# Fourteen column tiles of a gated unit laid between the steps of a paged sample attention

## The reference

```python
def decoder_layer(x, p, pos, past, lam_init, ...):
    h = rmsnorm(x, g_mix)
    z = h @ w_in
    q = z[..., :QK_COLS].reshape(B, T, N_HEADS, 2, HEAD_DK)
    ...
    gate_s = jax.nn.sigmoid(z[..., U_END + D_MODEL:])
    ...
        k_past, v_past, h0 = past
        segments = [(k_past, v_past, past_pos), (k, v, pos)]
    att = diff_attention(q, pos, segments, lam)
    att = rmsnorm(att, g_head) * (1.0 - lam_init)
    branch_a = att.reshape(B, T, ATTN_WIDTH) @ w_attn_up

    y_ssm, h_re, h_im = s5_scan(u, h0, ...)
    glu = jax.nn.gelu(y_ssm.reshape(B, T, SSM_WIDTH)) @ w_glu
    branch_s = glu[..., :D_MODEL] * jax.nn.sigmoid(glu[..., D_MODEL:])

    x = x + (gate_a * branch_a + gate_s * branch_s) @ w_out
    x = x + peer_ffn(...)
    x = x + (p @ w_ple) * jax.nn.sigmoid(rmsnorm(x, g_ple) @ w_ple_gate)
```

## Time and profile before

| | us |
|---|---|
| median of 3 runs (4792.35 to 4802.76) | 4796.71 |
| span of the profiled execution | 4793.1 |

### The profile page before, as it was taken

One profiled execution on the slowest core, in us unless ns is written; L12 is line 12 of the kernel. 1 busy time (PEld: TensorE's weight loads), 2 busy tenths in 40 slices (PEclk: granted clock), 3 DMA queues, 4 the chain that ended last, 5 costly groups with the idle time before them and its releaser, 6 DMA issues. The chain is left out here.

```text
span 4793.1 us, 80957 instructions
## 1 busy us (share of the span) xinstructions
PE 4433.3 (92%) x29778; PEld 4169.2 (87%) x29778; DVE 2599.0 (54%) x4336; ACT 1526.1 (32%) x2325; POOL 2545.3 (53%) x1827
## 2 busy tenths in 40 slices
PE   7999968998789898999999999999799999999999
PEld 6888857886379897999988999899799999999889
DVE  4477755453152302679565656555466666666631
ACT  3122214442143323223333333333333333333242
POOL 5688832321034342445566666666566666666543
PEclk9999978998789999999999999999899999999999
DMA  3222222336934432223688988878888888878532
GB/s 110 74 94 94 94 62 89 109 106 229 377 108 134 141 127 68 97 97 130 206 308 310 320 316 310 312 264 311 303 310 325 314 320 313 315 291 321 218 103 93
DMA packets 360238, 985.53 MB, mean 206 GB/s; under 512 B 43218, under 2 KB 120786, under 8 KB 301170
## 3 DMA queue, kind: packets, MB, share of 16 engines
q1 hardware_dynamic: 275138, 566.67, 34.7%
q0 software_dynamic: 47088, 339.37, 18.7%
q10 hardware_dynamic: 37824, 76.99, 4.2%
HBM read 901.03 MB, written 81.82 MB: 205 GB/s over the span
## 5 line engine op out<-in xcount | busy, mean ns | idle before, releaser
L2577 PE MATMUL val_y_ps<-val_wt,val_v 128*128 128x384 f32 x6144 | 1105.3, 338 | 39.2 <-DVE val_wt L2651 21.4
L247 PE MATMUL rt_acc<-xn_act,rt_w_hi 128*128 128x384 f32 x4096 | 1075.0, 343 | 64.0 <-POOL rt_w_rest L237 63.2
L2577 PEld LDWEIGHTS val_y_ps<-val_wt,val_v 128*128 128x128 f32 x6144 | 1065.7, 188 | 78.1 <-DVE out_xT L2675 56.4
L237 POOL TENSOR_TENSOR rt_w_rest<-rt_w_raw,rt_w_hi 128x512 fp32r<-128x512 f32 x576 | 743.4, 1311 | 562.4 <-ACT rt_w_hi L232 559.2
L247 PEld LDWEIGHTS rt_acc<-xn_act,rt_w_hi 128*128 128x128 f32 x4096 | 745.6, 190 | 87.8 <-POOL rt_w_rest L237 84.2
L2539 POOL TENSOR_TENSOR val_v<-val_v_raw,val_v 128x2048 fp32r<-128x2048 f32 x128 | 590.3, 4612 | 367.1 <-ACT val_v L2610 367.1
L247 PE MATMUL rt_acc<-xn_act,rt_w_rest 128*128 128x384 f32 x2048 | 697.0, 340 | 0.0
L232 ACT ACTIVATE rt_w_hi<-rt_w_raw 128x512 fp32r<-128x512 f32 x576 | 345.6, 630 | 494.4 <-DMA rt_w_raw<-in_peer_uT 329.5
L2454 DVE CUSTOM_DVE_ANT_0 rt_space<-rt_space,rt_mid 128x2048 f32<-128x2048 f32 x160 | 361.4, 2280 | 241.8 <-DMA rt_space<-in_peer_u,out_row_id 234.8
L2675 DVE TENSOR_TENSOR out_xT<-out_xT,val_y_ps 128x384 f32<-128x384 f32 x512 | 277.0, 551 | 376.6 <-PE val_y_ps L2577 376.6
L2610 ACT ACTIVATE val_v<-val_v_raw 128x2048 fp32r<-128x2048 f32 x128 | 245.4, 1918 | 583.6 <-PE val_y_ps L2577 551.6
(11 more groups left out here) (404 smaller groups left out, 7234.4 us busy)
## 6 DMA issues: line engine op xcount, KB each, us to landing
rt_w_raw<-in_peer_uT SPq DMA_DIRECT2D x512, 256.0 KB
val_v_raw<-in_peer_vp SPq DMA_DIRECT2D x128, 1024.0 KB, 4.9
scan_w_raw<-in_w_in SPq DMA_DIRECT2D x128, 256.0 KB, 3.0
pages_V<-in_cache_v SPq DMA_DIRECT2D x64, 512.0 KB, 11.8
att_w_raw<-in_w_in SPq DMA_DIRECT2D x96, 256.0 KB, 3.3
hid_scratch<-rt_hid ACTq DMA_DIRECT2D x128, 192.0 KB
gate_scratch<-rt_space ACTq DMA_DIRECT2D x12, 2048.0 KB
val_hid<-hid_scratch SPq DMA_DIRECT2D x32, 768.0 KB
```

The source lines that it names most:

```text
L237: e.tensor_tensor(self.rest[:, s, 0:nk, :], self.raw[:, s, 0:nk, :], self.hi[:, s, 0:nk, :].bitcast(F32), ALU.subtract).then_inc(self.rest ...
L247: mm = e.matmul(acc[:, h, 0:width], w[:, s, k, :], act[:, kt0 + k, a, col + h * width:col + (h + 1) * width], start=first and k == 0 and w ...
L2577: mm = e.matmul(y_ps[:, t % 2, 0:DW], v[:, c % 2, a, j, t * P:(t + 1) * P], wt[:, g % 2, j, b, :], start=j == 0 and a == 0 and b == 0, sto ...
```

## The change

The gated unit's products for column tiles 0 to 13 leave the mix stage and go between the steps of the sample attention; only tiles 14 and 15 (GLU_LATE = 2) stay. `stage_attention_sample` becomes `stage_sample_and_state`. Tile 0 goes ahead of the loop, each of its first six passes takes two tiles, the seventh one. In detail:

- The y tiles are read and split at the head of this stage, in a ring of four (`y_raw`), and later the same four buffers hold two gate tiles and two result tiles. `ys` outlives the stage.
- The two products of a tile now come as GATE, then VALUE, into one accumulator `acc`. ScalarE frees it after GATE (`open_gates`), VectorE after VALUE (`state_part`), both by `acc_free`. The scores lose their second buffer in PSUM for it.
- Weight units are issued by SP between the pages, in an order written out by hand, and split by ScalarE between its steps of the attention (`hi(u)` for unit u; unit u belongs to product u // 2).
- Keys and values share three buffers of 4 MB (`k.pages`) where there were four. Set 0 is the keys of sequence 0, then keys and values of the following sequences take turns; set m lies in buffer m % 3.
- The result of each early tile (128 x 544, 272 KB) is stored to `part_dram` and comes back in the mix stage (`load_back`) for its ATT product.
- The mix stage makes GATE 14, VALUE 14, GATE 15, VALUE 15 and then the 16 ATT products. All eight heads are normalised during the first four products, two heads in each (PAIRS = 4), and ATT 0 waits for them.

```diff
+GLU_LATE = 2
+GLU_EARLY = KT - GLU_LATE
...
+        y_raw = s.sb("y_raw", [P, 4, TOK])
+        gate, part = y_raw[:, 0:2], y_raw[:, 2:4]
+        ys = k.ys
+        S = s.ps("S", [P, 2, 512])
...
+        acc = s.ps("acc", [P, 2, 512])
...
+        def tiles(n):
+
+            return [2 * n + 1, 2 * n + 2] if n < NB - 2 else [2 * n + 1]
...
+        def keys_set(n):
+            return 2 * n - 1 if n else 0
+
+        def values_set(n):
+            return 2 * n + 2 if n < NB - 1 else 2 * n + 1
...
+            def load_y(t):
+                if t >= 4:
+                    e.wait_ge(y_rest, t - 3)
...
+            for t in range(4):
+                load_y(t)
+            for u in range(RING):
+                load_unit(u)
+            for t in range(4, CT):
+                load_y(t)
+            load_keys(1, range(NPG))
+            load_gate(0)
+            load_new(0)
+            load_values(0, range(NPG))
+            load_unit(4)
+            load_gate(1)
+            e.wait_ge(s_done, 1)
+            load_keys(2, range(0, 4))
+            load_unit(5)
+            load_keys(2, range(4, 8))
+            load_unit(6)
+            load_unit(7)
+            for n in range(NB - 1):
+                e.wait_ge(s_done, n + 2)
+                u = 8 * n + 4
+                load_unit(u + 4)
+                load_values(n + 1, range(0, 4))
+                load_unit(u + 5)
+                load_values(n + 1, range(4, 8))
+                if n:
+                    load_gate(2 * n + 1)
+                load_unit(u + 6)
+                load_unit(u + 7)
+                e.wait_ge(pv_done, n + 1)
+                load_new(n + 1)
+                load_unit(u + 8)
+                load_unit(u + 9)
+                if 2 * n + 2 < GLU_EARLY:
+                    load_gate(2 * n + 2)
+                if n + 3 < NB:
+                    load_keys(n + 3, range(0, 4))
+                load_unit(u + 10)
+                if n + 3 < NB:
+                    load_keys(n + 3, range(4, 8))
+                load_unit(u + 11)
...
+                e.wait_ge(acc_free, p + 1)
+                for v in range(U):
+                    w.multiply(e, 0, 0, p * U + v, acc, ys, v * UNIT, v == 0, v == U - 1)
...
+            e.wait_ge(y_rest, CT)
+            state_product(GATE, 0)
+            turn_weights(0)
+            state_product(VALUE, 0)
+            for n in range(NB - 1):
+                early, late = tiles(n)[0], tiles(n)[1:]
+                scores(n + 1)
+                state_product(GATE, early)
+                values(n)
+                state_product(VALUE, early)
+                turn(n)
+                for c in late:
+                    state_product(GATE, c)
+                turn_weights(n + 1)
+                for c in late:
+                    state_product(VALUE, c)
+            values(NB - 1)
...
+            def open_gates(c):
+                w.wait_used(e, 0, 0, (product(GATE, c) + 1) * U)
+                if c >= 2:
+                    e.wait_ge(part_stored[c % 2], 16 * (c // 2))
+                e.activation(halves(part[:, c % 2, :]), acc[:, :, 0:HALF], ACT.Sigmoid).then_inc(part_sig, 1)
+                e.wait_ge(part_sig, c + 1)
+                e.sem_inc(acc_free, 1)
+                e.wait_ge(gate_div, c + 1)
+                e.activation(gate[:, c % 2, :], gate[:, c % 2, :], ACT.Sigmoid).then_inc(gate_sig, 1)
...
+            for u in range(2):
+                hi(u)
+            for t in range(CT):
+                e.wait_ge(y_in[t % 4], 16 * (t // 4 + 1))
+                e.activation(ys[:, t, 0, :], y_raw[:, t % 4, :], ACT.Copy).then_inc(y_hi, 1)
+            hi(2)
+            hi(3)
+            exponents(0)
+            hi(4)
+            hi(5)
+            e.wait_ge(y_rest, CT)
+            open_gates(0)
+            copy_weights(0)
+            hi(6)
+            hi(7)
+            for n in range(NB - 1):
+                early, late = tiles(n)[0], tiles(n)[1:]
+                u = 8 * n + 4
+                exponents(n + 1)
+                store(early - 1)
+                hi(u + 4)
+                hi(u + 5)
+                open_gates(early)
+                copy_rows(n)
+                hi(u + 6)
+                hi(u + 7)
+                for c in late:
+                    hi(u + 8)
+                    store(early)
+                    hi(u + 9)
+                    open_gates(c)
+                copy_weights(n + 1)
+                for c in late:
+                    hi(u + 10)
+                    hi(u + 11)
...
+            def state_part(c):
+                w.wait_used(e, 0, 0, (product(VALUE, c) + 1) * U)
+                e.wait_ge(part_sig, c + 1)
+                x = halves(part[:, c % 2, :])
+                ch.step(e.tensor_tensor(x, acc[:, :, 0:HALF], x, ALU.mult))
+                e.sem_inc(acc_free, 1)
...
+        for c in range(GLU_EARLY, KT):
+            order += [(GATE, c), (VALUE, c)]
+        order += [(ATT, c) for c in range(KT)]
+        PAIRS = len(order) - KT
...
+        def load_back(e, c):
+            if c < GLU_EARLY:
+                if c >= 2:
+                    e.wait_ge(mix_ready, c - 1)
+                e.dma_start(back[:, c % 2, :], k.part_dram[c]).then_inc(back_in[c % 2], 16)
...
+            for n, (part, c) in enumerate(order):
+                if n == PAIRS:
+                    e.wait_ge(att_ready, NH)
+                e.wait_ge(part_read[n % 3], n // 3 + 1)
                 for v in range(U):
...
+                    if n < PAIRS:
+                        square_sum(n * U + v)
+                    w.multiply(e, 0, 0, n * U + v, acc[n % 3], k.att if part == ATT else ys, v * UNIT, v == 0, v == U - 1)
...
+                if n < PAIRS:
+                    for h in (n * U, n * U + 1):
+                        deviation(h)
+                        square(h + 2)
+                        if h:
+                            head_hi(h - 1)
+                elif n == PAIRS:
+                    head_hi(NH - 1)
```

359 lines of the change are left out of this document (197 added, 162 removed).

## The result

The changed kernel takes 4830.4 us (median of 6 runs, 4825.2 to 4835.5) against 4797.2 for the kernel before (6 runs on the same chip): 1.0067 of its time, 95% interval 1.0056 to 1.0078. It is slower by 0.7%, where 4766 us and "faster" had been predicted, and the time lies outside the range. The profiled span is 4823.4 us against 4793.1.

A forecast was written before the change was run, and what follows sets the result against it. Sample attention was taken as bound by pages, the mix stage by TensorE; new stage 318 us plus mix stage 152.6 make 470.6 against 501.2, 30.6 less, so 4766.1 us, range 4745 to 4790.

The forecast's parts named there:

- What bounds the kernel: Sample attention bound by page traffic at 408 GB/s, mix stage by TensorE; the new stage turns from DMA-bound to TensorE-bound.
- Start of the new stage: Sample attention up to the second scores: 55 us, with TensorE standing some 18 us before VALUE 0.
- A+47: Forecast start of VALUE 0, 47 us after the stage's start A (1150.8 us), once unit 5 has landed and been split.
- One sequence: Each of six sample-attention passes: 12.8 us of attention plus four products of 6.0, 36.8 us; with 0.8 of wait, 37.6.
- (1): In each sequence, ScalarE's second split waits for a unit issued behind four value pages; TensorE loses 0.8 us.
- (2): In each sequence, the gate tile behind all eight pages delays the output rows' copy; covered with 0.2 us to spare.
- K1: Keys of sequence 1; before the change, 4.19 MB took 13.9 us from issue at 1151.55 to first use at 1165.45.
- ScalarE's chain is later: Rival for the sequences: pages a tenth slower, waits grow, 3 us in each of seven, 4787 us; 15 in 100.
- TensorE's clock falls inside a sequence: Rival: 3.3 us lost per clock fall, 4792 us if once in each of eight sequences, 4819 if twice; eight in 100.
- A rule against the order on ScalarE: Two table loads per sequence at 1.28 us without the skill page's 1380 ns drain, which would add an estimated 11 us.
- The mix stage's head: Eight heads' norms on VectorE, 4.93 us each, first reciprocal at 7.9, delay the first attention product to 54.6 us.
- The output tiles: Sixteen attention products at 6.0 us plus 2.0 for the clock, 98 us; the wait for mix_ready costs nothing.

The follow-up runs named there:

- start_in_need: unit_and_gate_first with the start's gates opened before splits, and weight units 4 to 13 and gates issued ahead of later pages: 4775.7 us, 0.9951.
- unit_and_gate_first: Changed kernel with each turn's second weight unit and early gate tile both issued ahead of the value pages on SyncE: 4801.0 us, 1.0006.
- unit_first: Changed kernel with only each turn's second weight unit issued ahead of four value pages on SyncE: 4829.1 us, 1.0061.
- deviation_early: Changed kernel with the first root of the heads' norm ahead of the first four splits on ScalarE: 4833.1 us, 1.0070.
- all_orders: both_lists plus start units 4 to 9 ahead of later pages, first gates before splits, and two sums and roots first at the mix head: 4770.2 us, 0.9945.
- head_ordered: both_lists with the mix head's first root ahead of the splits and each next head's sum and root moved one slot earlier: 4765.6 us, 0.9938.
- gate_first: Changed kernel with the mix stage's gate sigmoid ahead of the splits for two tiles later, on ScalarE alone: 4806.5 us, 1.0016.
- back_later: Changed kernel with the mix stage's gate and part loads issued behind the next tile's weight loads, on SyncE alone: 4803.9 us, 1.0007.
- both_lists: Changed kernel with the edits of back_later and unit_and_gate_first together: 4774.7 us, 0.9951.

## Why the prediction was wrong

**What bounds the kernel: right.** The stage of the sample attention was bound by pages, the waits for pages are gone, and laid out well the sequences run at TensorE's speed.

**Start of the new stage: right in kind, 3 us short.** VALUE 0 starts at A+49.2 (A+47 was said), TensorE idle for 19.9 us before it, ScalarE released by unit 5 (1200.22, table load 1200.87, sigmoid 1202.16). I took this idle time as given, because the lists stood so in the diff; start_in_need shows that it was the order of the lists and not the 11.6 MB.

**One sequence: the step that failed is waits (1) and (2).** Both were found and both were sized with the 408 GB/s of a window inside a burst, from its first byte, and with nothing but the bytes issued ahead. The burst begins at 262 GB/s for 5 us, and 0.7 MB more than those bytes had moved when the unit was there. The unit behind four pages was split 11.6 us after the end of scores (1268.87 less 1253.19 and 4.05), where 8.9 had been said, and the sigmoid behind the gate tile began at 18.2 (1275.47), where 15.7 had been said. That turned 0.8 us of wait into 2.3 to 3.5. The rest is the clock, which the sum had at nothing here: it falls to 0.50 in or just behind each of these waits, and VALUE then takes 7.5 to 8.8 us instead of 6.0. The six waits are 16.1 us, and the six sequences are 27.7 us longer than the 224.5 of unit_and_gate_first: the other 11.6 are the clock. The slow start could have been read before: the prediction's own row of K1 has 4.19 MB in 13.9 us, where 2 us and 408 GB/s give 12.3. The prediction said of (2) that anything beyond its 0.2 us to spare would be paid six times; unit_first showed exactly that, once (1) no longer stood in front of it.

**The rivals.** The second, "ScalarE's chain is later", is what happened in this stage, with its reason nearly as given: 26.6 us against its 21. It had 15 in 100, but the argument against it (the DMA engines have been idle before each burst) didn't hold: behind such a pause the rate is 262 GB/s and not 408. The third, "TensorE's clock falls inside a sequence", came about in part, 1.4 to 2.8 us in each, but not by itself: in unit_and_gate_first the same small matmuls stand between the same products, and the clock is 1.00 for 225 us. What pulled it down was the wait. The changed kernel's mean over the six sequences is 0.95, just at the limit that the prediction had named as the sign of this rival. The Trainium skill (TensorE: Matmul & The Clock Gate, HAM oscillation) describes this loss for a loop whose waits come back in each pass; the trace agrees, with 0.80 in the wait and 0.50 behind it.

**A rule against the order on ScalarE: weighed rightly.** The table loads in the new stage take 1.28 us and stand 0.02 us behind the split (1269.52 behind 1268.87 and 0.63). The drain of 1380 ns for each switch that the Trainium skill gives (ScalarE: Activation LUTs, What ACT_TABLE_LOAD costs) shows in none of the rows.

**The mix stage's head: right, 3 us short.** 57.9 against 54.6. A head's pitch on VectorE was 5.05 us, not 4.93, and the first reciprocal started 9.9 us in, not 7.9, because ScalarE waited for the third and fourth unit before the first root. deviation_early, all_orders and head_ordered bear out the chain: it is moved only when all three engines' lists move.

**The output tiles: the step that failed outright.** "The unit behind the wait for mix_ready still lands 3 us before its split's result is wanted: nothing." For TensorE alone that holds: in gate_first, where SyncE's list is as it was, TensorE is busy for 99.39 of the tiles' 99.40 us. But the split is not only work for TensorE's sake: on ScalarE the opening of the gate stands behind it, and the addition that SyncE waits for stands behind that. I followed the added wait to the engine that multiplies and stopped there, instead of asking who else stands behind each instruction that it delays. It costs 22.7 us on 98, nearly a quarter; in the traces of back_later and gate_first 22.1 and 21.3 of them come back, each cut alone.

With both failed steps mended, both_lists has 4775 us, 9 above the 4766 of the prediction, which is about what the other rows of the first table miss (3.1 + 2.3 + 3.3). What I didn't ask was whether the order could be put right: that gave another 22 us.

## What to carry to other kernels

When a change adds a wait to an engine's list, follow it round until it comes back: list what stands behind the waiting instruction, what each of those delays on its own engine, and stop only where the chain ends or closes. If it closes, its length is the pitch, however idle each engine in it looks. In a queue of transfers, small loads that are wanted soon belong ahead of big ones that are wanted late, and all of them at once: with two late loads, moving either one shows nothing. And time the landing of what follows a burst from the burst's first microseconds, not from its middle, and don't count on the bytes issued ahead of it being all that moves before it is there.

## What the runs showed of the hardware

Waits of 2.3 to 3.5 us in the middle of steady matmuls, with TensorE busy before them, were each followed by a granted clock of 0.50 for 3.4 to 6.8 us (the changed kernel, six times). In three of the six the clock fell within the wait, in the other three 0.7 to 1.2 us after TensorE had gone on. A burst of 512 KB pages into idle DMA engines, counted from its first issue, moves 262 GB/s in its first 5 us, 379 in the next 6 and about 400 then; the first burst in this stage of the kernel before has 268 in the 5 us from 1152. A reciprocal of 128x544 takes VectorE 3.55 us, where a multiplication of the same shape takes 0.72. And profiled runs of the same code had drifted apart by up to 7.6 us when they came to this stage, 1150 us into the span, so a gain of 5 us could be told by the stage's own length in the trace, not by the time of the whole.
